# Strassen's identity for the lower half of the MLP's down products, with two weight sums made by VectorE

## The reference, cut to what matters

```
def sq_relu_mlp(h, w1, w2):          # h 256x2048, w1 2048x8192, w2 8192x2048
    a = jax.nn.relu(h @ w1)
    return (a * a) @ w2
```

## Time and profile before

| | us |
|---|---|
| median of three runs | 2084.14 |
| the profiled execution's own time | 2084.32 |
| its span, first to last instruction | 2082.5 |
| TensorE busy | 2074.2 (100%) |
| VectorE busy | 1580.3 (76%) |
| ScalarE busy | 1170.2 (56%) |
| granted TensorE clock, mean | 1.00 |

### The profile page before, as it was taken

How to read it: one execution, slowest core, us unless ns; L and a number is a source line. 1 busy time by engine, 2 the same in 40 slices (tenths; PEclk the granted TensorE clock), 3 DMA queues, 4 the chain that set the end, 5 groups by cost and what they waited for, 6 DMA issues and landing times.

```text
span 2082.5 us, 27541 instructions
## 1 busy us (share of the span) xinstructions
PE 2074.2 (100%) x10802; PEld 1756.7 (84%) x10802; DVE 1580.3 (76%) x2105; ACT 1170.2 (56%) x1442; POOL 80.0 (4%) x74
## 2 busy tenths in 40 slices
PE   9999999999999999999999999999999999999999
PEld 8888888888888888888788888888888888888887
DVE  7798787778778877668887777656778677677777
ACT  6777475565564555665656655554445445454454
POOL 0000000000000000000010210000000000000000
PEclk9999999999999999999999999999999999999999
DMA  8565555564554644447587876455687688588677
GB/s 326 195 233 195 199 213 189 203 215 169 209 190 160 238 167 150 159 148 237 190 287 201 249 231 203 185 182 214 203 261 251 203 262 242 212 236 242 240 207 218
DMA packets 71746, 443.28 MB, mean 213 GB/s; under 512 B 7872, under 2 KB 14784, under 8 KB 20288
## 3 DMA queue, kind: packets, MB, share of 16 engines
q1 hardware_dynamic: 64992, 393.28, 51.4%
q0 software_dynamic: 6624, 48.24, 12.5%
HBM read 437.16 MB, written 4.33 MB: 212 GB/s over the span
## 4 chain that ended last, share of the span: by engine, by line
PE 89%; DVE 4%; ACT 1%; POOL 1%; issue 1%; DVEq 0%; ACTq 0%
PE bank L1230 25%; PE bank L1235 13%; PE bank L1253 12%; PE bank L1255 12%; PE bank L1257 12%; PE bank L1269 3%; PE bank L1271 3%; PE bank L1273 3%; DVE wlo L2004 2%; POOL SM L2730 1%; DVE W L2603 1%; PE bank L1360 1%; PE bank L1496 1%; PE bank L1432 1%; DVE W L2622 1%
## 5 line engine op out<-in xcount | busy, mean ns | idle before, releaser
L2004 DVE TENSOR_TENSOR wlo<-raw,whi 128x2048 fp32r<-128x2048 f32 x305 | 697.8, 2288 | 189.5 <-ACT whi L1556 157.7
L1556 ACT ACTIVATE whi<-raw 128x2048 fp32r<-128x2048 f32 x305 | 583.3, 1913 | 233.7 <-PE bank L1257 201.5
L1230 PE MATMUL bank<-A,whi 128*128 128x512 f32 x2448 | 586.8, 392 | 0.4 <-ACT whi L1556 0.4
L1230 PEld LDWEIGHTS bank<-A,whi 128*128 128x128 f32 x2448 | 451.5, 188 | 90.7 <-issue 1.9
L1235 PEld LDWEIGHTS bank<-A,wlo 128*128 128x128 f32 x2432 | 311.9, 191 | 11.8
L1235 PE MATMUL bank<-A,wlo 128*128 128x256 f32 x2432 | 315.4, 283 | 0.0
L1253 PE MATMUL bank<-whi,A2h 128*128 128x512 f32 x736 | 289.1, 393 | 0.0
L1255 PE MATMUL bank<-whi,A2l 128*128 128x512 f32 x736 | 287.0, 390 | 0.0
L1257 PE MATMUL bank<-wlo,A2h 128*128 128x512 f32 x736 | 286.8, 390 | 0.0
L1253 PE MATMUL bank<-whi,A 128*128 128x512 f32 x512 | 203.5, 397 | 0.1
L1255 PE MATMUL bank<-whi,A 128*128 128x512 f32 x512 | 200.0, 391 | 0.2
(11 more groups left out here) (273 smaller groups left out, 2190.4 us busy)
## 6 DMA issues: line engine op xcount, KB each, us to landing
raw<-wst SPq DMA_DIRECT2D x300, 1024.0 KB, 4.9
W<-wst SPq DMA_DIRECT2D x35, 1024.0 KB, 6.8
W<-wst POOLq DMA_DIRECT2D x29, 1024.0 KB, 8.7
XR<-wst POOLq DMA_DIRECT2D x12, 1024.0 KB, 8.2
W<-cum_scratch SPq DMA_DIRECT2D x8, 1024.0 KB, 6.9
XR<-wst SPq DMA_DIRECT2D x6, 1024.0 KB, 7.5
W<-rows SPq DMA_DIRECT2D x21, 256.0 KB, 5.7
raw<-wst POOLq DMA_DIRECT2D x5, 1024.0 KB, 9.0
```

Of the source, the lines that this page charges most:

```text
L1230: last = e.matmul(o[:, :], whi[:, s, k * P:(k + 1) * P], A1[:, k, :, :].rearrange("p h t -> p (h t)"), start=k == 0, stop=packed and k == ...
L1556: e.activation(whi[:, u % 3, :], raw_of(u), ACT.Copy).then_inc(*hi.inc((u, 3)))
L2004: e.tensor_tensor(wlo[:, u % 3, :], raw_of(u), whi[:, u % 3, :], ALU.subtract).then_inc(*lo.inc((u, 3)))
```

## The change

For quarters 1, 2 and 3 the lower 8 hidden tiles also go by Strassen's identity for both pairs of blocks (tags `dl`), with mixes of their own (`low mix`). The upper halves of quarters 0, 1 and 2 stay with Strassen (`dp`); the last quarter's upper half becomes 8 plain B units, which end the kernel. Quarter 0 keeps 8 B units for its lower half. So quarters 1 and 2 have 28 P and no B units, quarters 0 and 3 have 14 P and 8 B units as before. The order of a set is a c b d e f g, and in quarters 1 to 3 two sets stand between 8 `up` units as `-a-cb-de-f-ga-cb-de-fg`.

In all sets of the MLP d and g are now made by VectorE's `add`, as in `bp`; b and f stay with the adding DMA. d and f are accumulated by TensorE on a's PSUM bank, so the copy of a by ScalarE and two additions in SBUF per set go: a set has nine drains by VectorE, all from PSUM, in place of eleven. In the sets of quarters 1 to 3 every product has a bank of its own. The two parts of a mix (four operations; roundings and subtractions) stand behind two successive units. The diff, cut to its core:

```
+def summed_in_flight(tag):
+    return tag[0] == "np"
 def products(tag):
-    top, low = (8, 12) if tag[0] in ("bp", "np") else (16 * tag[1] + 8, 16 * tag[1] + 12)
+    top, low = ((8, 12) if tag[0] in ("bp", "np") else (16 * tag[1], 16 * tag[1] + 4) if tag[0] == "dl" else
+                (16 * tag[1] + 8, 16 * tag[1] + 12))
-    four = tag[0] in ("np", "dp")
+    four = summed_in_flight(tag)
...
+    def both(kind, s):
+        return sevens(kind, "mlp_w2_2", s, 0) + sevens(kind, "mlp_w2_2", s, 1)
+    plains, sets, order = [], [], ""
     for s in range(QT):
...
+        plains += [("A", ("up", s, i), "mlp_w1_2", (16 * s + i) * P) for i in range(0 if s else 4, 16)] + down(s)
+        sets += both("dl", s) if s else []
+        sets += both("dp", s) if s < QT - 1 else []
+        eight = "-a-cb-de-f-ga-cb-de-fg"
+        if s == 0:
+            order += 12 * "-" + "-a-c-b-d-e-f-g-"
+        else:
+            order += "-a-c-b-d-e-f-g-" if s == 1 else eight
+            order += eight
+    u += in_turn(order, sets, plains)
...
+LEFT = ((1, 0, 2, 3),) + ((),) * (QT - 2) + ((0, 1, 2, 3),)
...
     for s in range(QT):
-        after[at["up", s, 15] + 1].append(("mix", s))
+        for part in range(2):
+            if s < QT - 1:
+                after[at["up", s, 15] + 1 + part].append(("mix", s, part))
+            if s:
+                after[at["up", s, 8] + part].append(("low mix", s, part))
...
 # sums(): as before for bp, now for dp and dl too
     if name(u + 2) == "a":
         yield ("acc", unit(u + 2, "b"))
-    if u + 3 < len(units) and units[u + 3][1][0] in ("np", "dp"):
+    if u + 3 < len(units) and units[u + 3][0] == "P" and summed_in_flight(units[u + 3][1]):
         return
     if name(u + 3) in ("d", "g"):
         yield ("add", u + 3)
     if name(u + 3) == "d":
         yield ("acc", unit(u + 3, "f"))
...
 # drains()
+    if tag[0] in ("dp", "dl"):
+        return {"a": ((0, left, 1),), "b": ((1, right, 1), (0, right, 1)), "c": ((0, right, 1),), "d": ((0, right, -1),),
+                "e": ((0, left, 1),), "f": ((1, right, -1), (1, left, 1)), "g": ((1, left, 1),)}[tag[3]]
...
 # product_block(), TensorE
+                if tag[0] in ("dp", "dl"):
+                    if name in "df":
+                        w.wait_ge(*evac_v((product(u, "a" if name == "d" else "d"), 0)))
+                    opens = name in "ab" or name in "ceg" and alone(tag)
...
 # low_mixed(), VectorE (ScalarE's has the four roundings in part 1)
+                if part == 0:
+                    for i in range(8):
+                        w.wait_ge(*up_v("l", at["up", s, i]))
...
+                    e.tensor_tensor(a22, a21, a22, ALU.subtract).then_inc(*low_v.inc("1", s))
...
+                for name, high, low, x in low_parts():
+                    w.wait_ge(*low_a("h" + name, s))
+                    e.tensor_tensor(low, x, high, ALU.subtract).then_inc(*low_v.inc("l" + name, s))
...
 # acc(), GpSimd
-                if units[u][1][3] == "f" and units[u][1][0] == "bp":
+                if units[u][1][3] == "f" and not summed_in_flight(units[u][1]):
                     w.wait_ge(*add_v(product(u, "d")))
```

More of the change, by code:

```diff
@@ L163, in plan, with down, plain, alone @@
     u += b(("upb",), "mlp_w1_2", 0)
-    def down(s, nbs):
-        return [("B", ("down", s, nb, i), "mlp_w2_2", 16 * s + 4 * i, nb * 512) for nb in nbs
-                for i in range(2 if seven(s, nb) else 4)]
-    for s in range(QT):
[L170 to L176, removed]
-    return u
-def seven(s, nb):
-    return s < QT and nb < ND
+    def down(s):
+        return [("B", ("down", s, nb, i), "mlp_w2_2", 16 * s + 4 * i, nb * 512) for nb in LEFT[s] for i in plain(s)]
+    def both(kind, s):
+        return sevens(kind, "mlp_w2_2", s, 0) + sevens(kind, "mlp_w2_2", s, 1)
+    plains, sets, order = [], [], ""
+    for s in range(QT):
+        plains += [("A", ("up", s, i), "mlp_w1_2", (16 * s + i) * P) for i in range(0 if s else 4, 16)] + down(s)
[8 more added lines that the diff above has]
+    u += in_turn(order, sets, plains)
+    return u
+LEFT = ((1, 0, 2, 3),) + ((),) * (QT - 2) + ((0, 1, 2, 3),)
+def plain(s):
+    return (2, 3) if s else (0, 1)
+def alone(tag):
+    return tag[0] in ("dp", "dl") and tag[1] > 0
 def timetable(units):
@@ L226, in timetable @@
     run(("r2",), at["nv", 0, 3], 7)
-    after[at["bo", 2, 0]].append(("mix", -1))
+    after[at["bo", 2, 0]] += [("mix", -1, part) for part in range(2)]
     for j in range(KVH):
@@ L232, in timetable @@
             run(("na", 0), at["nq", 0, 3] + 1, 9)
-            after[at["nv", 0, 3] + 5].append(("mix", MIX_HEADS))
+            after[at["nv", 0, 3] + 5] += [("mix", MIX_HEADS, part) for part in range(2)]
             continue
@@ L373, in block_of @@
     left, right = pair_of(tag)
+    if name in "adf":
+        return tag[:3]
+    if alone(tag):
+        return (u,)
     return {"c": (s, right, 0), "e": (s, left, 0), "g": (s, left, 1)}.get(name, (u,))
@@ L483, in last_read @@
             name = units[u][1][3] if units[u][0] == "P" else None
-            if units[u][1][0] in ("np", "dp") and name == "e":
+            if name == "e" and summed_in_flight(units[u][1]):
                 return u
@@ L913, in stack_kernel, with kept, hidden @@
         xu = W[:, W_XU:W_XU + T]
[L915 to L923, removed]
+        def kept():
+            return W[:, W_KT:W_KT + 512]
+        def hidden(s, i):
+            c = M_MIX + (i - 8) * T if i >= 8 else M_H + (i if s else i % 4) * T
             return W[:, c:c + T]
@@ L1063, in load @@
                         w.wait_ge(*lo((split, 3)))
-                        if name == "e" and units[before][1][0] == "bp":
+                        if name == "e" and not summed_in_flight(units[before][1]):
                             w.wait_ge(*add_v(product(before, "g")))
@@ L1261, in product_block @@
             def product_block(u, o):
-                name = units[u][1][3]
+                tag, name = units[u][1], units[u][1][3]
+                if tag[0] in ("dp", "dl"):
+                    if name in "df":
+                        w.wait_ge(*evac_v((product(u, "a" if name == "d" else "d"), 0)))
+                    opens = name in "ab" or name in "ceg" and alone(tag)
+                else:
+                    opens = name in "abdf"
+                goes_on = tag[0] in ("dp", "dl") and name in "df"
                 for k in range(4):
@@ L1285, in factor @@
                 if name in "aeg":
-                    i, t = (8 if name == "a" else 12) + k, int(name == "g")
+                    i, t = (8 if name == "a" else 12) + k - (8 if kind == "dl" else 0), int(name == "g")
                     c = slice(t * P, (t + 1) * P)
@@ L1298, in factor @@
                 which = {"b": "1", "c": "4", "d": "2", "f": "3"}[name]
+                if kind == "dl":
+                    return h, low, (low_a("h" + which, s), low_v("l" + which, s))
                 return h, low, (mix_a("h" + which, mix_round(s)), mix_v("l" + which, mix_round(s)))
@@ L1944, in na_high, with low_mixed, mixed @@
                              ACT.Copy).then_inc(*na_a.inc(f"h{h}", j))
-            def mixed(s):
+            def low_mixed(s, part):
+                if part == 0:
+                    return
+                w.wait_ge(*mm_done(at["dp", s - 1, 1, "f"]))
+                for name, high, _, x in low_parts():
+                    w.wait_ge(*low_v(name, s))
+                    e.activation(high, x, ACT.Copy).then_inc(*low_a.inc("h" + name, s))
+            def mixed(s, part):
+                if part == 0:
+                    return
+                if s > 0:
+                    w.wait_ge(*mm_done(at["dl", s, 1, "f"]))
                 for name, high, _, x in parts_of(s):
@@ L2035, in mixed @@
                     e.tensor_tensor(to, x, y, op).then_inc(*mix_v.inc(name, mix_round(s)))
-                for name, high, low, x in parts_of(s):
-                    w.wait_ge(*mix_a("h" + name, mix_round(s)))
-                    e.tensor_tensor(low, x, high, ALU.subtract).then_inc(*mix_v.inc("l" + name, mix_round(s)))
             def heads_drained(u, n):
```

99 lines of the change are left out of this document (61 added, 38 removed).

## The result

The changed kernel takes **2142.33 us** (median of four runs, 2142.13 to 2143.68) against 2083.94 us for the kernel before in the same comparison (2083.45 to 2084.37): a ratio of 1.0279, 95% interval 1.0266 to 1.0291, 58.4 us more. The forecast was 2126.6, 42.5 more: the direction and the two terms of the loss held, and 15.9 us were missing from it, because the adding DMA of f, which had no term, was late too. That 2142.3 still lies in the range is in part luck, since its upper end was set for other things: errors per unit, and a b that lands at 10.5 us.

What follows compares the result with a forecast made beforehand. The prediction took TensorE's number of matmuls to bound the kernel, with VectorE's reserve in question. It summed -10.3 + 31.8 + 21.0 = +42.5 us on 2084.1 to 2126.6 us, range 2094 to 2146.

Steps and rivals of the forecast that it cites:

- the two terms of the loss: In the five MLP blocks: TensorE waits 31.8 us for VectorE, and 21.0 us more for the adding DMA of b.
- TensorE saves 10.3 us: Quarters 1 and 2 each swap 8 B units for 14 P units, taking 10.3 us from TensorE.
- The handover of a sum, 6.58 us; the blocks +31.8: Sum, rounding, split take VectorE 6.58 us; the blocks need 450.5 us against TensorE's 415, less 3.7 lead: +31.8.
- The adding DMA of b, +21.0: In the MLP's sets b's DMA lands after 8.7 us, too late for VectorE: 18.0 in second halves, 3.0 in first.
- The DMA of f ... hidden: In the MLP's sets f's DMA starts after d's sum with 13.8 us of units before it is needed: no cost.
- No two adding DMAs of the new order start within 10 us: In the new order adding DMAs stand well apart, so the median landing of 8.7 us was taken, not 11.8.
- Small edits, cost nothing: Mix order, sums in quarter 0, loads, drains and banks add no time; if cover fails, at most 2.3 us.
- The second rival: Adding DMAs land later, as in pairs, at 11.8 us, delaying the ten b: 2158 to 2172 us, 10%.
- TensorE's waits, forecast 53 us: In the MLP waits rise from 0 to 53 us, nearly all for VectorE's split, on b, d, e and g.
- a granted clock that leaves 1.00: Named sign that the prediction is wrong; no row shows what the clock does after waits of 2 us.
- Rival C: Raised with the experiments: TensorE's clock falls after the new waits and costs the missing time, under 16 us; no chance given.
- Last 8 B units, quarter 0: The last 8 B units, 5.46 us each beside one split of 2.2, and quarter 0 are without waits.

Runs made afterwards that it cites:

- e9_interleaved: The changed kernel with sums and f's DMA issued one unit earlier and the two sets of a half side by side: 2081.48 us, ratio 0.9986 to the kernel before.
- e2: The changed kernel with the MLP's b and f DMAs storing instead of adding, so those sums are left out: 2106.99 us, ratio 1.0105 to the kernel before.
- e1: The changed kernel with VectorE's sums and f's DMA in the MLP's sets issued one unit earlier: 2106.25 us, ratio 1.0100 to the kernel before.
- e4: The changed kernel with sums and f's DMA one unit earlier, and b and f stored instead of added: 2083.54 us, ratio 0.9995 to the kernel before.
- e6: The changed kernel with SP's weight loads cut to 128 of 2048 columns beside the adding DMAs: 2126.02 us, ratio 1.0197 to the kernel before.

## Why the prediction was right, and where it was not

- **TensorE saves 10.3 us.** 48 matmuls fewer, as counted. The full amount was never seen as time: from the first `up` unit of the MLP's quarter 0 to the end of the span, e9_interleaved (2080.8 - 1436.5) is 5.0 us shorter than the kernel before (2082.5 - 1433.2), because its blocks last 84.1 us on average in place of 83. Nine waits there are 1.5 us in all; the rest is in the P units' matmuls, which start 0.236 us apart on average (waits included) in place of 0.228. Why, no run shows.
- **The handover of a sum, 6.58 us; the blocks +31.8.** Right: 6.54 us in the trace. e2, which has in the main this term and the saving, stands at +21.8, 19.8 without the attention's 2, against +21.5; its blocks at +31.1 against +31.8.
- **The adding DMA of b, +21.0.** Right in place, and near in size. ScalarE waits for it at b (38.0 us over nine times in the blocks). With the sums early, storing in place of adding gives back 22.2 us (e1 against e4), and there b is the only adding DMA that ScalarE waits for. With all landings at about 8 us the total is +41.3 (e6) against +42.5. On the forecast's own scale (6.5 us for 0.9 us of landing) 8.1 us make the term 4.3 smaller, and the attention adds 2, which gives +40.2: 1.1 us short.
- **"The DMA of f ... hidden": this step failed.** It had 13.8 us of units by TensorE's reckoning, but its start is set by d's sum on VectorE, which is itself late, and its landing was 10.4 and not 8.7 us. I had looked for other *adding* DMAs within 10 us ("No two adding DMAs of the new order start within 10 us"), and not for SP's loads, which the new order puts 2.3 to 2.9 us ahead of it. Measured: VectorE's splits of f come 13.2 us late in all, and in e6 the blocks are 16.6 us shorter, of which up to 3.5 are b's, whose DMAs of the second halves land that much sooner.
- **A row misread.** The forecast takes 11.8 us (1667.92 to 1679.75) for the landing of an adding DMA with a neighbour. In the trace of before that DMA lands after 8.6 us; the rounding at 1679.75 waits for a load that SP issued at 1669.74. The late one is the second of the pair, issued at 1673.24, 3.5 us behind a load and 5.3 us behind the first: 12.1 us. Its like stands at 1502.05, 1844.78 and 2015.69 (11.6 to 12.3 us), so the trace of before already had adding DMAs that land late close behind other transfers. SP, GpSimd and ScalarE there:

```profile
1669.74 0.33 SPq L1068 DMA_DIRECT2D raw<-wst  x1
```
```profile
1673.24 0.86 POOL L2780 DMA_DIRECT2D W<-wst  x1 [4.46 <-ACT whi L1556]
```
```profile
1685.32 1.92 ACT L1556 ACTIVATE whi<-W 128x2048 fp32r<-128x2048 f32 x1 [3.65 <-DMA W<-wst]
```
- **"Small edits, cost nothing": 2 to 2.6 us.** The order of a mix delays attention; TensorE had "no wait" there, but ScalarE did, and so did what follows it. The loads were miscounted beside it: of 18 per block 14 are on SP's queue and 4 are the adding ones, and 18 of 1 MB in 83 us are 227 GB/s and not 217; nothing rests on it.
- The two together: 13.9 in the blocks and 2.0 in the attention are the 15.9 that were missing. In the blocks f's 13.2 and b's 3.7 us are 3.0 more than that, so the forecast's other terms together were about that much too large; which of them, I can't say.
- **The second rival** had the right kind of mechanism (adding DMAs that land later) on the wrong transfer, b, whose median landing stayed at 8.7, and with the wrong neighbour, another adding DMA in place of SP's loads.
- **TensorE's waits, forecast 53 us.** The view shows 36.7 us for the two kinds, while the blocks are 66.7 us longer than 415. The remainder, 29 us, is in slow matmuls, 17 us of it where the granted clock is 0.50, the lower of its two levels, 1.2 GHz: behind a wait of 1.66 us they start 0.43 us apart instead of 0.23, for 3.4 us:

```profile
1702.48 0.69 PE L1319 MATMUL bank<-wlo,A2h 128*128 128x512 f32 x1 [1.66 <-DVE wlo L2061]
1702.97 0.63 PE L1315 MATMUL bank<-whi,A2h 128*128 128x512 f32 x1
1703.40 0.63 PE L1317 MATMUL bank<-whi,A2l 128*128 128x512 f32 x1
...
1705.96 0.43 PE L1317 MATMUL bank<-whi,A2l 128*128 128x512 f32 x1
1706.23 0.40 PE L1319 MATMUL bank<-wlo,A2h 128*128 128x512 f32 x1
```

  The forecast had named a granted clock that leaves 1.00 as a sign of being wrong, and it came: 0.95 to 0.98 in the blocks. Rival C says that this costs the missing time. The chain that ended last, asked for the five blocks alone, speaks against it:

```profile
by line: DMA raw<-wst 19.8%; issue 17.2%; DVE wlo L2061 13.3%; ACT whi L1604 13.1%; DMA W<-wst 12.8%; DVE W L2072 9.4%; DVE XR L2028 3.0%; PE bank L1269 1.6%; DVE W L2202 1.3%; DVE W L2115 1.2%; PE bank L1319 1.1%; PE bank L1274 0.8%; PE ba
```

  It is on TensorE for 24.4 of 481.7 us, nearly all of it at 1800.55 to 1804.31, 1995.22 to 2013.26 and behind 2090.67, and the clock is at its lower level in 6.1 us of these. At half speed that is at most 3.1 us of the 58.4, an estimate from these rows. The other slow matmuls stand off the chain. The four runs of the change agree: the mean clock was 0.992, 0.995, 0.995 and 0.997, and the times 2142.13, 2142.45, 2142.21 and 2143.68 us, so a higher clock was no faster. No run changed the clock alone, so up to 3 us stay open.
- **Last 8 B units, quarter 0.** Right: from the first `up` of quarter 0 to the start of the blocks 176.75 us pass before (1433.21 to 1609.96) and after (1434.61 to 1611.36).

## What to carry to other kernels

When units get shorter, price the longest chain across engines (sum, rounding, split, and the DMA that the sum releases), not each engine's total: here the same VectorE work costs 58 us as it stood, 21 when its sums are issued one unit earlier, and nothing when the two sets also stand side by side. A DMA is hidden only if both its start and its landing are; take its landing with the loads that will be running at its start, of every queue. And an order that is "the same work" on an engine in order, such as which rounding comes first, has a price at each place where a helper is shared.

## What the runs showed of the hardware

An adding DMA of 1 MB, SBUF and DRAM, issued by GpSimd, lands after 8.0 us with little traffic beside it (e6), 8.7 us ahead of other loads, 10.4 us when two loads of 1 MB were issued 2.3 to 2.9 us before it (8.0 us when it was one load, 2.4 us before), and 12.4 us when two were issued 0.2 to 0.8 us before it, at an average traffic below that of the kernel before. A storing one on the same queue lands after 5.0 us (e4) and takes 0.53 us to issue in place of 0.86; in e2, issued just behind the loads as in the change, f's took 7.0 us. GpSimd's issue took 0.86 to 0.88 us in the blocks, while VectorE was busy for 86% of them.

The Trainium skill, "DMA: Bandwidth & Descriptors", section "Anatomy of one DMA — SWDGE (gpsimd) path", gives 4.4 us for 1 MB by its fit, an estimate. The storing DMA alone is near it (5.0 us), the adding one is not, with or without neighbours. The Trainium skill, "SBUF — State Buffer", section "SBUF: two separate sides", has VectorE and GpSimd lock each other out of a shared pair of ports only while VectorE works in a 2-port mode or, with two inputs in SBUF, while GpSimd reads SBUF. VectorE's splits and sums here have two inputs in SBUF, and the issue times of 0.86 to 0.88 us show no delay by them.
